# One Trainium2 core, a hybrid decoder layer: identity products in waits, upper expert weights loaded by halves, the output projection's second half in two passes, routing picks in pairs

## The chip, the cores and the metric

The kernel runs on one core of one Trainium2 chip. The metric is device time in microseconds (us) of one execution, the median of three. Lower is better. TensorE multiplies and transposes, VectorE (DVE) and ScalarE (ACT) work element by element, GpSimd (POOL) here adds and gathers rows by indirect transfers, and SyncE (SP) issues all other transfers in one queue.

## What is computed

One pre-norm decoder layer on 512 tokens of 1024 channels, in float32. Cut to what matters here:

```python
h = rmsnorm(x, g_mix); proj = h @ w_in            # attention, convolution, mLSTM and gates
merged = gate0*(y_att@w_br_att) + gate1*(y_conv@w_br_conv) + gate2*(y_m@w_br_mlstm)
x = x + merged @ w_out
h2 = rmsnorm(x, g_ffn)
lg = h2 @ w_router_g + b_router_g                 # top 1 of 4 groups
le = h2 @ w_router_e + b_router_e                 # top 2 of the 8 experts in it
x = x + moe(h2)                                   # 32 experts, 256 hidden, silu(x@gate)*(x@up) @ down
x = x + sigmoid(rmsnorm(x, g_ple) @ w_ple_gate) * (p @ w_ple_proj)
return rmsnorm(x, g_final)
```

## The kernel before, in words

Each engine has one hand-written program, and the engines meet at counting semaphores. Every engine runs strictly in its written order, so a wait holds all that stands behind it. Tokens are in T = 4 tiles of P = 128, channels in KD = 8 tiles. A float32 operand of a large product is split in a rounded high part and a remainder, and three products (high x high, low x high, high x low) replace one. ScalarE rounds, VectorE makes the remainder. A plain float32 product shows as two TensorE instructions in the profile.

**Start.** Token tiles are normed (`normed_tile`, VectorE L1679), transposed on TensorE (L1113) into eight PSUM banks, rounded by ScalarE (`h_rounding`, L713) and split by VectorE (`h_remainder`, L1687). `first_column_tile` then does its three groups of eight products, the last group on the remainders.

**Projection `merged @ w_out`.** `project(i)` makes tile `i % 4` of column half `i // 4` in 24 products: for each of three parts (merged high x weight high, merged high x weight remainder, merged remainder x weight high) eight channel tiles. VectorE adds the result to x (`add_x2`, L2012). `turn_half(i - 1)`, four transposes, and `router(i - 1)`, four products with the router's weights, stand inside the 24 products of tile i. Between them VectorE's `h2_half` (L2022) copies the transposed piece out of PSUM and multiplies it by `g_ffn`. ScalarE squares each half row and takes the root (L977, L982).

**Routing.** For each token tile VectorE forms the reciprocal root (`row_root`), then `pick(t)`: logits, best group, the two best experts, their one-hot rows `oh` and their sum `tmp`. `ranked` turns counts from TensorE (`RANKS`, `LAST_RANKS`) into places in the experts' blocks, and `hits` makes the table of token numbers. GpSimd gathers the rows by that table. `constant_products` are products of the identity with itself. Five 512-wide products stand before `HIT_WEIGHT`, the table of weights.

**Experts.** For n = 0 to 31: `up(n)` (16 products on 2 MB of weights), `turn_block(n + 1)` (four transposes of gathered rows, L1505), `expert_down(n - 1)` (1 MB of weights). Weights lie in a ring of RING = 7 slots for up and 9 for down. A slot is given back when its product is done (`up_done`, `down_done`), and SP then issues the next load into it:

```python
            for n in range(RING, NEXP):
                if DOWN_RING <= n < IN_ORDER:
                    sp.wait_ge(down_done, n + 1 - DOWN_RING)
                    down_weights(n)
                sp.wait_ge(up_done, n + 1 - RING)
                up_weights(n)
```

The slots lie over memory that earlier stages use. Slot 4 of up lies over `merged_low`, and slot 3 of down over channel tiles 4 to 7 of the second half's weight remainder, `wo_low[1]`. Before, both are loaded after the projection's last tile, from L569 and L572.

**Tail.** The per-layer embedding's products, the sum of the experts' rows read back, and two more norms.

Of the kernel before, what the change touches and what calls it, by code (L numbers as in the profile page):

```python
# [28 lines left out]
F32 = mybir.dt.float32  # L29
# [94 lines left out]
def build(nc, x, consts, chan, g_mix, r_bias, g_final, w_cm, w_tm, w_if, w_gate, w_branch, w_out,  # L124
# [5 lines left out]
    with ExitStack() as ctx:  # L130
# [115 lines left out]
        DOWN_RING, IN_ORDER = len(down_w), 20  # L246

# [61 lines left out]
        best_at = sb("best_at", [P, 8], mybir.dt.uint32)  # L309
        best_index = sb("best_index", [P, 8])  # L310
# [58 lines left out]
        w_if_split = sem("w_if_split")  # L369
        if_projected = sem("if_projected")  # L370
# [5 lines left out]
        columns_read = sem("columns_read")  # L376
# [14 lines left out]
        tm_done = sem("tm_done")  # L391
# [111 lines left out]
        def _(sp):  # L503
# [19 lines left out]
            def token_weights(r):  # L523

                sp.wait_ge(if_projected, 1)
                sp.dma_start(wtm, w_tm[r, :, :, :]).then_inc(tm_loaded, 16)
# [28 lines left out]
            sp.wait_ge(tm_done, ROUNDS * T)  # L555
# [39 lines left out]
            up_weights(3)  # L595

# [13 lines left out]
            down_weights(3)  # L610
            down_weights(4)
            up_weights_in_halves(4)
# [5 lines left out]
            for n in range(RING, NEXP):  # L618
# [3 lines left out]
                sp.wait_ge(up_done, n + 1 - RING)  # L622
                up_weights(n)
# [54 lines left out]
        def _(act):  # L678
# [48 lines left out]
            def forget_gate():  # L727

                act.wait_ge(if_projected, 1)
# [86 lines left out]
            def token_out(r, u):  # L816
                act.wait_ge(tm_done, r * T + u + 1)
# [154 lines left out]
            for i in range(2 * T):  # L972
                t, total = i % T, (square_halves, ss2)[i // T]
                act.wait_ge(x2_ready, i + 1 + (i == 2 * T - 1))
                if i:
                    act.wait_ge(x2_squared, i)
                act.activation(junk2, x_sb[:, t, i // T * 512:(i // T + 1) * 512], ACT.Square,  # L977
                               accum_out=total[:, t:t + 1]).then_inc(x2_squared, 1)
                if i >= T:
                    act.wait_ge(x2_squared, i + 1)  # L980
                    act.wait_ge(mean_ready, 1)
                    act.activation(rr2[:, t:t + 1], ss2[:, t:t + 1], ACT.Sqrt, scale=1.0 / D,  # L982
                                   bias=mean_halves[:, t:t + 1]).then_inc(rooted, 1)
            act.wait_ge(picked, T)
# [110 lines left out]
        def _(pe):  # L1095
# [13 lines left out]
            for t in range(T):  # L1109
                pe.wait_ge(x_normed, t + 1)  # L1110
# [21 lines left out]
            def gates():  # L1132

                pe.wait_ge(w_if_split, 1)
# [3 lines left out]
                last.then_inc(if_projected, 1)  # L1138
# [20 lines left out]
            def token_tile(r, u, first=0, end=KD):  # L1159
# [9 lines left out]
                if end == KD:  # L1169
                    last.then_inc(tm_done, 1)  # L1170
# [100 lines left out]
            def units(r):  # L1271

                if r == 0:
                    pe.wait_ge(columns_read, 1)
# [86 lines left out]

            def project(i, first=0, end=3 * KD):
# [5 lines left out]
                if i == T:  # L1368
                    pe.wait_ge(rounded, WO_REST_ROUNDED + KD)
                for n, (part, k) in list(enumerate(last_tile_last if i == 0 else by_part))[first:end]:  # L1370
# [6 lines left out]
                    if i == T and n == KD:  # L1377
# [3 lines left out]
                              n == 0, n == 3 * KD - 1)  # L1381
                if end == 3 * KD:
# [37 lines left out]
            pe.wait_ge(params_loaded, 32)  # L1420
            pe.wait_ge(gate_read, 3 * KD)
            project(0)
            for i in range(1, T + 1):
# [4 lines left out]
                project(i, 10)  # L1428
            for i in range(T + 1, 2 * T):
                project(i, 0, 4)  # L1430
                turn_half(i - 1)
                if i < 2 * T - 1:
                    project(i, 4, 10)
                else:
                    project(i, 4, 8)
                    pe.wait_ge(picked, 2)
                    mm(RANKS, const("upper"), tmp[:, 0:2, :], True, False)
                    mm(RANKS[:, NEXP:], ones, tmp[:, 0, :], False, True).then_inc(routing_mm, 1)
                    project(i, 8, 10)
                router(i - 1)  # L1440
                project(i, 10)
# [8 lines left out]
            constant_products(1)  # L1450
# [10 lines left out]
            pe.wait_ge(picked, 3)  # L1461
            mm(LAST_RANKS[:, NEXP:], ones, tmp[:, 2, :], False, False)
# [13 lines left out]
            pe.wait_ge(picked, T + 1)  # L1476
# [973 lines left out]
```

## Time and profile before

| | |
|---|---|
| median of 3 runs | 933.99 us (933.07 to 936.02) |
| the profiled execution's own time | 939.01 us |
| its span, first to last instruction | 937.1 us |
| TensorE busy | 896.6 us (96%) |
| VectorE busy | 503.9 us (54%) |
| ScalarE busy | 343.3 us (37%) |
| GpSimd busy | 195.6 us (21%) |
| mean granted TensorE clock | 0.988 |
| bytes moved | 180.35 MB, mean 192 GB/s |

The 1.9 us between the profiled time and its span lie outside the first and last instruction. TensorE's busy time is a modelled one: an engine shown busy can still run at the low clock or wait within a group. Rates of 410 to 430 GB/s are the highest that the core's transfers reach in the page's 40 slices.

### The profile page before, as it was taken

The numbers are of one execution on the slowest core, as the hardware profiler recorded it, in microseconds if no ns is written. First come the engines' busy times: TensorE is split into PE (matmuls) and PEld (weight loads), VectorE is DVE, ScalarE is ACT, GpSimd is POOL, SyncE is SP. The second block draws the span as 40 slices with busy tenths as digits, with TensorE's granted clock in tenths as the row PEclk, the third lists the DMA queues.
The fourth block names the chain that finished last, engine by engine and source line by source line (L and its number), as shares of the span: only waits on it lengthen the run. The fifth ranks groups of instructions, "written<-read, shape, count | busy, mean of one in ns | idle before, by whom it ended". The sixth has DMA issues, their size and how long they took to land. (4 is left out here: it accounts for less than half of the span.)

```text
span 937.1 us, 12264 instructions
## 1 busy us (share of the span) xinstructions
PE 896.6 (96%) x4816; PEld 658.4 (70%) x4816; DVE 503.9 (54%) x1043; ACT 343.3 (37%) x571; POOL 195.6 (21%) x169
## 2 busy tenths in 40 slices
PE   5999999999999999999999999998999999879896
PEld 4778778878877887888888888874555555434586
DVE  6368679759767999943333336474112112111766
ACT  5534453535355357622222243111122122112465
POOL 0052253327134433000000000001333332221000
PEclk9999999999999999999999999998999999999899
DMA  7430321121131111551222219969999999999701
GB/s 278 168 103 23 114 80 54 58 101 57 35 113 45 46 56 46 213 177 73 85 94 101 101 37 395 355 228 349 421 419 422 420 417 421 418 422 393 270 23 68
DMA packets 28801, 180.35 MB, mean 192 GB/s; under 512 B 5808, under 2 KB 6320, under 8 KB 17992
## 3 DMA queue, kind: packets, MB, share of 16 engines
q1 hardware_dynamic: 23624, 171.16, 46.3%
q0 software_dynamic: 5120, 8.41, 2.4%
q8 instruction: 39, 0.64, 0.3%
q14 instruction: 18, 0.15, 0.0%
HBM read 175.33 MB, written 12.59 MB: 201 GB/s over the span
## 5 line engine op out<-in xcount | busy, mean ns | idle before, releaser
L1097 PE MATMUL bank<-mT_parts,low_parts 128*128 128x512 f32 (+1 forms) x456 | 178.5, 394 | 0.0
L1097 PE MATMUL bank<-arena,cst 128*64 128x256 f32 (+2 forms) x918 | 135.9, 437 | 8.8 <-DMA arena<-in_w_expert 7.2
L1097 PE MATMUL bank<-mT_parts,x_parts 128*128 128x512 f32 (+1 forms) x328 | 132.7, 405 | 2.7 <-DVE arena L1766 2.3
L1097 PE MATMUL bank<-hT_parts,x_parts 128*128 128x512 f32 (+1 forms) x328 | 129.1, 394 | 0.0
L1701 DVE TENSOR_TENSOR low_parts<-arena,x_parts 128x1024 fp32r<-128x1024 f32 (+1 forms) x44 | 64.6, 1470 | 93.8 <-ACT x_parts L707 93.4
L2183 DVE TENSOR_TENSOR cst<-bank,chn 128x512 f32<-128x512 f32 x32 | 22.1, 692 | 168.1 <-PE bank L1505 168.1
L1097 PEld LDWEIGHTS bank<-arena,cst 128*64 128x64 f32 (+1 forms) x918 | 64.4, 141 | 64.6 <-issue 31.6
L1097 PEld LDWEIGHTS bank<-mT_parts,low_parts 128*128 128x128 f32 (+1 forms) x456 | 85.0, 186 | 21.2
L1753 DVE SCALAR_TENSOR_TENSOR arena<-arena,chn 128x512 f32<-128x512 f32 x116 | 99.1, 912 | 0.0
L2334 POOL DMA_INDIRECT mT<-x_rows,table x32 | 33.0, 1031 | 270.5 <-DVE table L2113 257.6
L1097 PE MATMUL bank<-arena 128*128 128x64 f32 (+9 forms) x400 | 79.8, 332 | 0.0
L1097 PEld LDWEIGHTS bank<-mT_parts,x_parts 128*128 128x128 f32 (+1 forms) x328 | 61.0, 186 | 19.6 <-DVE low_parts L1701 3.5
L2319 POOL TENSOR_TENSOR arena<-arena 128x128 f32<-128x128 f32 (+3 forms) x32 | 38.6, 1207 | 172.8 <-ACT arena L803 172.8
L1097 PEld LDWEIGHTS bank<-hT_parts,x_parts 128*128 128x128 f32 (+1 forms) x328 | 61.0, 186 | 15.3 <-issue 1.0
L1097 PEld LDWEIGHTS bank<-arena 128*128 128x128 f32 (+1 forms) x400 | 56.4, 189 | 19.6 <-issue 13.6
L2340 POOL DMA_INDIRECT expert_rows<-mT,table x32 | 32.4, 1013 | 152.0 <-ACT mT L1005 147.5
L803 ACT ACTIVATE arena<-arena,small 128x384 f32<-128x384 f32 (+3 forms) x32 | 32.6, 1020 | 56.9 <-DVE small L1853 56.9
L1097 PE MATMUL bank<-mT_parts,cm_high_b 128*128 128x512 f32 x128 | 52.4, 419 | 0.0
L948 ACT ACTIVATE arena<-bank 128x512 f32<-128x512 f32 x24 | 14.2, 595 | 101.6 <-PE bank L1097 94.6
L1097 PE MATMUL bank<-hT_parts,cm_high_b 128*128 128x512 f32 x128 | 49.2, 393 | 0.0
L1005 ACT ACTIVATE mT<-bank,table_weight 128x512 f32<-128x512 f32 x32 | 22.0, 687 | 67.0 <-PE bank L1097 67.0
L1097 PE MATMUL bank<-x_parts,mT_parts 128*128 128x384 f32 x128 | 44.8, 350 | 0.0
(303 smaller groups left out, 1582.0 us busy)
## 6 DMA issues: line engine op xcount, KB each, us to landing
arena<-in_w_expert SPq DMA_DIRECT2D x21, 2048.0 KB, 26.8
arena<-in_w_expert SPq DMA_DIRECT2D x26, 1024.0 KB, 23.9
arena<-in_w_cm SPq DMA_DIRECT2D x32, 512.0 KB, 3.5
arena<-in_w_gate SPq DMA_DIRECT2D x7, 1536.0 KB, 6.5
yT<-in_w_expert SPq DMA_DIRECT2D x5, 2048.0 KB, 23.2
hT<-in_w_expert SPq DMA_DIRECT2D x4, 2048.0 KB, 25.1
arena<-in_w_tm SPq DMA_DIRECT2D x4, 1536.0 KB, 6.9
arena<-in_w_branch SPq DMA_DIRECT2D x8, 768.0 KB, 7.8
```

Source lines behind the costliest of these rows:

```text
L803: act.activation(sc[:, u % 2, 0:n], sc[:, u % 2, 0:n], ACT.Exp, bias=nmx[:, u % 2:u % 2 + 1], accum_out=den[:, u:u + 1]).then_inc(exps_don ...
L948: act.activation(sgm[:, br], (PA, PB, S_16)[br][:, :], ACT.Sigmoid).then_inc(gate_read, 1)
L1005: act.activation(yr[slot], Y[b2][:, :], ACT.Copy, scale=table_w(0, n)).then_inc(y_scaled, 1)
L1097: return pe.matmul(out, lhsT, rhs, start=start, stop=stop)
L1701: dve.tensor_tensor(low, weights, high.bitcast(F32), ALU.subtract).then_inc(done, 1)
L1753: dve.scalar_tensor_tensor(cacc[:, j % 2], ypad[:, j:j + SEQ], weight, cacc[:, j % 2], ALU.mult, ALU.add).then_inc(conv_step, 1)
L2183: dve.tensor_tensor(xT[b2], TR[:, :].rearrange("p (k h s) -> p k h s", k=KD // 2, h=2), chn[:, G_FFN:G_FFN + KD].rearrange("p (h k) -> p k ...
L2319: pool.tensor_tensor(dst[:, 0:n], sc[:, u % 2, 0:n], sc[:, u % 2, n:2 * n], ALU.add).then_inc(pool_step, 1)
L2334: pool.indirect_dma_start(out=xr[slot], out_offset=None, in_=x2_halves, in_offset=bass.IndirectOffsetOnAxis(ap=token_halves, axis=0), boun ...
L2340: pool.indirect_dma_start(out=expert_halves, out_offset=bass.IndirectOffsetOnAxis(ap=row_halves, axis=0), in_=yr[slot], in_offset=None, bo ...
```

## The change

Six edits. (1) Before the transposes of token tiles 0 to 2, TensorE does 7, 6 and 3 identity products; 8 stand before the first `turn_block`, 4 behind it, and `constant_products(1)` before the last router becomes 2. (2) The second column half of the projection runs in two passes over its four tiles: first the 12 products that read `merged_low` and `wo_low[1]`'s upper half, then the other 12. `up_weights(4)` and `down_weights(3)` are issued behind the first pass. (3) Loads 7, 8 and 9 of the up ring are issued by halves, the first half when the first half of `up(0)`, `up(1)`, `up(2)` is done. (4) The transposed pieces are copied by ScalarE without a factor; `g_ffn` is multiplied once into the router's weights by VectorE, in the merge stage. (5) `pick` and `row_roots` handle two token tiles at a time: 0 and 1, then 2 and 3, the latter behind the last router. (6) The `RANKS` products move from the middle of the last projection tile to behind it, ahead of the last `turn_half`, and one product of `LAST_RANKS` moves behind `picked`.

```diff
             pe.wait_ge(ident_loaded, 16)
             for t in range(T):
+                for q in range((7, 6, 3, 0)[t]):
+                    mm(MM[:, 0:P], ident, ident)
                 pe.wait_ge(x_normed, t + 1)
...
+            low_first = [(2, k) for k in range(KD)] + [(1, k) for k in range(KD // 2, KD)]
+            second_half = low_first + [(1, k) for k in range(KD // 2)] + [(0, k) for k in range(KD)]
+            LOW = len(low_first)
...
-                project(i, 10)
+                project(i, 10, LOW if i == T else 3 * KD)
             for i in range(T + 1, 2 * T):
-                project(i, 0, 4)
-                turn_half(i - 1)
-                if i < 2 * T - 1:
-                    project(i, 4, 10)
-                else:
-                    project(i, 4, 8)
-                    pe.wait_ge(picked, 2)
-                    mm(RANKS, const("upper"), tmp[:, 0:2, :], True, False)
-                    mm(RANKS[:, NEXP:], ones, tmp[:, 0, :], False, True).then_inc(routing_mm, 1)
-                    project(i, 8, 10)
-                router(i - 1)
-                project(i, 10)
+                project(i, 0, LOW)
+            project(T, LOW)
+            project(T + 1, LOW, LOW + 5)
+            turn_half(T)
+            project(T + 1, LOW + 5)
+            project(T + 2, LOW, LOW + 1)
+            router(T)
...
+            project(T + 3, LOW + 5, LOW + 10)
+            pe.wait_ge(columns_then_logits_read, 2)
+            router(T + 2)
+            project(T + 3, LOW + 10)
+            pe.wait_ge(picked, 2)
+            mm(RANKS, const("upper"), tmp[:, 0:2, :], True, False)
+            mm(RANKS[:, NEXP:], ones, tmp[:, 0, :], False, True).then_inc(routing_mm, 1)
             constant_products(2)
             turn_half(2 * T - 1)
-            constant_products(1)
+            constant_products(2)
             router(2 * T - 1)
...
+            constant_products(8)
             turn_block(0, 0, rows_gathered[0], 16, first=True)
+            constant_products(4)
```

SyncE's part and the marks on TensorE:

```diff
+        IN_HALVES_FROM = (0, 1, 2)
+        IN_HALVES = (5,) + tuple(n + RING for n in IN_HALVES_FROM)
...
             def up_weights_in_halves(n):
                 for half in range(2):
+                    if n >= RING:
+                        sp.wait_ge(*((tm_then_up_half_done, ROUNDS * T + n + 1 - RING), (up_done, n + 1 - RING))[half])
...
             up_weights(2)
             up_weights(3)
+            sp.wait_ge(if_then_low_projected, 2)
+            up_weights(4)
+            down_weights(3)
...
-                sp.wait_ge(up_done, n + 1 - RING)
-                up_weights(n)
+                if n in IN_HALVES:
+                    up_weights_in_halves(n)
+                else:
+                    sp.wait_ge(up_done, n + 1 - RING)
+                    up_weights(n)
```

ScalarE's order for the last piece, and VectorE's for the pairs:

```diff
+            x2_square(2 * T - 1)
+            turned_copy(2 * T - 1, 0, 2, OUT, 2 * T)
+            x2_root(2 * T - 1)
+            turned_copy(2 * T - 1, 2, 4, S_16, 2 * T + 1)
...
-            for t in range(T - 1):
-                h2_half(T + t)
-                row_root(t)
-                if t == T - 2:
-                    ranked(0, RANKS, 1)
-                pick(t, lambda: add_x2(T + t + 1))
+            add_x2(T + 1)
+            row_roots(0)
+            add_x2(T + 2)
+            pick(0, lambda: add_x2(T + 3))
...
-            h2_half(2 * T - 1)
-            row_root(T - 1)
-            pick(T - 1, lambda: None)
+            ranked(0, RANKS, 1)
+            row_roots(T - 2)
+            pick(T - 2, lambda: None)
```

In the paired `pick` the reductions, the copy of the indices, the one-hot rows and `tmp` take both tiles in one instruction. The logits, the comparison with the best group, its one-hot row, the masked logits, the best eight and their indices stay one instruction for each tile.

## Rows read from the trace of the kernel before

**Rows 1.** The trace by windows: busy time of each engine, clock, transfers.

```profile
618.00:620.00 2.00, 2.00 (x14) 1.78 (x14) 1.80 (x7) 0.00 (x0) 0.00 (x0) 1.00 0.00 0
638.00:640.00 2.00, 1.00 (x4) 0.60 (x4) 0.11 (x1) 0.00 (x0) 0.00 (x0) 0.76 1.04 412
...
646.00:648.00 2.00, 1.50 (x14) 0.75 (x10) 0.47 (x1) 1.01 (x1) 0.00 (x0) 1.00 0.28 68
700.00:800.00 100.00, 100.00 (x718) 51.66 (x716) 18.36 (x47) 21.30 (x48) 32.69 (x32) 1.00 1.01 420
```

**Rows 2.** Timeline of the experts in mid-stage: start, duration, instruction.

```profile
691.23 0.66 PE L1505 MATMUL bank<-cst,mT 128*128 128x128 f32 x4
697.55 0.66 PE L1505 MATMUL bank<-cst,mT 128*128 128x128 f32 x4
```

**Rows 3.** Timeline of SP, its load issues around the experts' start.

```profile
593.89 0.80 SPq L564 DMA_DIRECT2D arena<-in_w_expert  x2
...
624.97 3.33 SPq L569 DMA_DIRECT2D arena<-in_w_expert  x4
...
646.94 0.33 SPq L564 DMA_DIRECT2D arena<-in_w_expert  x1
```

**Rows 4.** Timeline of the start, transposes and first column tile.

```profile
2.09 0.43 SPq L509 DMA_DIRECT2D cst<-in_consts  x1
...
9.09 1.94 PE L1113 MATMUL bank<-cst,arena 128*128 128x128 f32 x8 [9.09 <-DVE arena L1679]
...
15.11 3.67 PE L1113 MATMUL bank<-cst,arena 128*128 128x128 f32 x16 [0.81 <-DVE arena L1679]
...
18.70 3.24 PE L1097 MATMUL bank<-mT_parts,cm_high_b 128*128 128x512 f32 x8
...
19.69 2.47 DVE L1687 TENSOR_TENSOR hT_parts<-bank,mT_parts 128x512 fp32r<-128x512 f32 x4
...
23.65 2.03 PE L1097 MATMUL bank<-hT_parts,cm_high_b 128*128 128x512 f32 x8
```

**Rows 5.** Timeline of the last projection tile and last pick.

```profile
617.14 0.53 PE L1097 MATMUL bank<-tmp,cst 128*128 128x64 f32 x4
...
622.47 0.75 DVE L2012 TENSOR_TENSOR x_sb<-x_sb,bank 128x256 f32<-128x256 f32 x2 [0.59 <-PE bank L1097]
622.95 0.77 PE L1405 MATMUL bank<-cst,x_sb 128*128 128x128 f32 x4
...
624.01 0.29 ACT L982 ACTIVATE small<-small 128x1 f32<-128x1 f32 x1
...
625.44 0.25 DVE L2059 SCALAR_TENSOR_TENSOR rl<-bank,small,r_b 128x36 f32<-128x36 f32 x1
...
626.38 0.23 DVE L2063 TENSOR_SCALAR t<-rl,per 128x4 f32<-128x4 f32 x1
626.51 0.22 DVE L2066 TENSOR_SCALAR oh<-oh,per 128x4 f32<-128x4 f32 x1
...
628.00 0.25 DVE L2075 SCALAR_TENSOR_TENSOR tmp<-cst,best_index,oh 128x32 f32<-128x32 f32 x1
...
628.31 0.43 PE L1097 MATMUL bank<-tmp,cst 128*128 128x64 f32 x2 [0.82 <-DVE tmp L2075]
```

**Rows 6.** The page's groups, ScalarE's copy of a bank.

```profile
L948 ACT ACTIVATE arena<-bank 128x512 f32<-128x512 f32 x24 | 14.2, 595 | 101.6 <-PE bank L1097 94.6
```

**Rows 7.** Timeline from the routing's fillers to expert 1.

```profile
631.44 4.54 PE L1097 MATMUL bank<-cst 128*128 128x512 f32 x10
...
635.91 1.15 PE L1097 MATMUL bank<-mT,cst 128*64 128x64 f32 x32
...
638.85 1.00 PE L1505 MATMUL bank<-cst,mT 128*128 128x128 f32 x4 [1.79 <-DMA mT<-x_rows,table]
...
640.73 6.18 PE L1097 MATMUL bank<-arena,cst 128*64 128x256 f32 x32 [0.88 <-DVE cst L2183]
...
648.37 1.95 PE L1097 MATMUL bank<-yT,cst 128*64 128x256 f32 x16 [0.88 <-DVE cst L2183]
```

More of the change, by code:

```diff
@@ L246, in build, with up_count @@
         DOWN_RING, IN_ORDER = len(down_w), 20
+        IN_HALVES_FROM = (0, 1, 2)
+        IN_HALVES = (5,) + tuple(n + RING for n in IN_HALVES_FROM)
+        def up_count(n):
+            return sum(16 * (1 + (m in IN_HALVES)) for m in range(n % RING, n + 1, RING))
         CM_LOADS = 2 * ROUNDS * 16
@@ L971, in _, with x2_square @@
             wo_rounding(1, 0, KD)
-            for i in range(2 * T):
+            def x2_square(i):
                 t, total = i % T, (square_halves, ss2)[i // T]
@@ L978, in _, with x2_root, turned_copy @@
                                accum_out=total[:, t:t + 1]).then_inc(x2_squared, 1)
-                if i >= T:
[L980 to L984, printed above, removed]
+            def x2_root(i):
+                t = i - T
+                act.wait_ge(x2_squared, i + 1)
+                act.wait_ge(mean_ready, 1)
+                act.activation(rr2[:, t:t + 1], ss2[:, t:t + 1], ACT.Sqrt, scale=1.0 / D,
+                               bias=mean_halves[:, t:t + 1]).then_inc(rooted, 1)
+            def turned_copy(i, first, end, bank, count):
+                act.wait_ge(x2_turned, count)
+                if i and first == 0:
+                    act.wait_ge(logits_done, i)
+                act.activation(h2_piece[:, first:end, :], bank[:, 0:(end - first) * P].rearrange("p (k s) -> p k s", k=end - first),
+                               ACT.Copy).then_inc(h2_ready, 1)
+            for i in range(2 * T - 1):
+                x2_square(i)
+                turned_copy(i, 0, 4, (S_16, OUT)[i % 2], i + 1)
+                if i >= T:
+                    x2_root(i)
+            x2_square(2 * T - 1)
+            turned_copy(2 * T - 1, 0, 2, OUT, 2 * T)
+            x2_root(2 * T - 1)
+            turned_copy(2 * T - 1, 2, 4, S_16, 2 * T + 1)
+            act.wait_ge(picked, 3)
             act.activation(t4[:, :, :], t4[:, :, :], ACT.Exp).then_inc(act_step, 1)
@@ L1367, in project @@
                     pe.wait_ge(x2_ready, i - 3)
-                if i == T:
+                if i == T and first == 0:
                     pe.wait_ge(rounded, WO_REST_ROUNDED + KD)
-                for n, (part, k) in list(enumerate(last_tile_last if i == 0 else by_part))[first:end]:
+                order = second_half if i >= T else last_tile_last if i == 0 else by_part
+                for n, (part, k) in list(enumerate(order))[first:end]:
                     if i == 0 and part == 0:
@@ L1381, in project @@
                               n == 0, n == 3 * KD - 1)
+                if i == 2 * T - 1 and end == LOW:
+                    last.then_inc(if_then_low_projected, 1)
                 if end == 3 * KD:
@@ L1476, in _ @@
             pe.wait_ge(picked, T + 1)
+            mm(LAST_RANKS[:, NEXP:], ones, tmp[:, 2, :], False, False)
             mm(LAST_RANKS, const("upper"), tmp[:, 2:T, :], False, True).then_inc(routing_mm, 1)
@@ L1512, in up @@
                 for k in range(KD):
+                    if k == KD // 2 and in_halves:
+                        last.then_inc(tm_then_up_half_done, 1)
                     if k == KD // 2 and between:
```

164 lines of the change are left out of this document (97 added, 67 removed).

## The prediction

> **What bounds the kernel now.** I read three views in turn: the busy shares, the trace by windows, and the timelines of the three places that the change touches. TensorE is busy for 96% of the span, so up to the experts whatever shortens TensorE's line shortens the kernel. In the experts' stage it is the loads: over 700 to 800 us transfers run at 420 GB/s with nothing to spare [rows 1]. An expert needs 3 MB (2 for up, 1 for down), some 7.5 us at that rate, while TensorE takes one expert every 6.32 us [rows 2]. TensorE lives on the slots filled in advance and must run out of them. So the end of that stage is fixed by when the stream of loads starts to run without a break, and not by when TensorE starts. The reader should see in [rows 1] two holes in the stream: none moved at 618 to 620, and 68 GB/s at 646 to 648. In the second, all slots were full and SP could issue nothing before up(0) had ended; the next load goes out at 646.94 [rows 3]. That instant is the one to follow. All loads before it are worth nothing, as long as they have landed by then.
>
> **The start.** Sixteen transposes take 3.67 us in the start [rows 4], 0.23 each, where four take 0.66 with their tail in mid-stage [rows 2], and the first eight products of the first column tile take 3.24 against 2.03 for the last eight [rows 4]. TensorE is at the low of its two clocks, 1.2 GHz, until some 21 us; the window rows do not say so there, the durations do. Ten fillers of 512 columns take 4.54 us [rows 7], so an instruction of 128 columns costs some 0.11 and an identity product, two such, 0.21 at the high clock and 0.43 at the low one. Seven products can begin once the identity is there (issued at 2.09), in front of the transposes of 9.09. If they bring the high clock, VectorE's last remainder, which ends at 19.69 + 2.47 = 22.16 [rows 4], becomes what the third group waits for: its last four products take 1.0, and with the second group in front the tile ends near 23.6 instead of 23.65 + 2.03 = 25.7, less a tail of 0.2. **Gain 1.9.** Lower bound none, if the clock rises no earlier.
>
> **First column half.** ScalarE copies the transposed pieces in place of VectorE. A copy of 512 columns takes 0.60 [rows 6]. ScalarE must square the half row first, and for tile 0 it is still rounding weights, so the first router waits some 0.25; the later ones have room. VectorE's new product on the router's weights lies in the merge stage, under TensorE's work: nothing; without that cover it would be some 0.4. **Cost 0.25.**
>
> **Second half and the pair.** The same number of products runs. Moving RANKS out of the last tile takes some 0.4 out ahead of the last add (four instructions, 0.53 with tail [rows 5]), which then ends at 622.47 + 0.75 - 0.4 = 622.8. But TensorE now waits for pick(0)'s tmp before the last transposes, and pick(0) puts that add in its middle: behind it come two one-hot operations and tmp, three steps of some 0.2, so 623.45. Then RANKS 0.4 and two identity products 0.4: the last transposes start at 624.25 instead of 622.95 [rows 5]. What is late next is ScalarE. It copies half a piece (between half and all of 0.60 [rows 6]; I take 0.4) and only then takes the root: at 625.15 instead of 624.01 [rows 5]. The reciprocal root has one operation more, 0.2, so the last pick starts 1.3 late, at 626.75 instead of 625.44.
>
> In the pick, an operation that waits for none follows in 0.13 (626.38 to 626.51 [rows 5]); a chained one costs 0.2 to 0.3. Added are five unchained seconds (0.65), two instructions for the second index search (0.25), one chained step for the first half's logits (0.3), and the second one-hot operation in front of tmp (0.2): 1.4. tmp starts at 628.00 + 2.7, and a product of 0.1 stands behind it ahead of the ranks. The table of tokens, the gathers and HIT_WEIGHT are all 2.85 late. **Cost 2.85**, bounds 2.0 (the pairs overlap more) and 3.6 (every added operation at 0.25).
>
> The Trainium skill (ScalarE: Activation LUTs, What ACT_TABLE_LOAD costs) gives a copy with immediate scale 186 ns plus 0.833 ns a column. For 512 columns that is 0.61 and [rows 6] agree; for 256 it is 0.40, the value taken between the bounds above. At the bound of 0.60 the cost would be 3.05.
>
> **Start of the experts.** HIT_WEIGHT ended at 637.06 [rows 7], now at 639.9. Eight products take 1.7, to 641.6, just the time at which the gathered rows would come if they need as long as before (638.85 + 2.85). So the eight products hide in that wait. If the rows come earlier, because the stream is empty then, the products cost what they overhang, at most 1.7, but nothing is gained either, since they stand in line in front. The transposes fell into a low clock: 0.76 over 638 to 640 [rows 1], 1.00 for four against 0.66, and up(0) took 6.18 against twice 1.95 [rows 7]. With the waits filled, up(0) starts at 641.7 + 1.88 - 0.34 = 643.25 and its first half ends at 645.2. In the start's time, 645.2 - 1.9 + 0.25 = 643.55. SP issues half of load 7 then: 3.4 before 646.94.
>
> **The loads put forward.** up 4 and down 3 go out behind the first pass, near 606.5 (593.89 plus the last turn and router of the first half and 48 products of 0.23), not at 624.97 and after [rows 3]. Without that, some 7.5 MB issued from 623.7 on would end at 643 or later and hold the stream; with it, 4.5 MB are left and end near 635. It gains nothing by itself; it lets the earlier release count. On SP's queue the two stand ahead of the stores of x2, which wait for VectorE anyhow until 610. On the freed stream half a slot of 1 MB lasts 2.5 us, and the next halves come a little late once: **cost 0.35.** Later releases follow TensorE, itself 1.5 earlier. **Gain of the release 3.05 in all**, start, first half and routing included.
>
> **The term that I cannot read off.** While VectorE does the longer pick, TensorE has only the ranks of two tiles, hits(0, 2) and three products. Before, it idled 0.82 there [rows 5]; now 0.82 + 1.4 for the pair and some 0.3 for ScalarE's root coming behind the copy: 2.5 us. In the trace an idle stretch of 1.79 was followed by the low clock [rows 7], and the next was 4 us of work at low clock, which cost up(0) 2.3 us. Behind the new gap stand hits, totals and five long fillers that end exactly when HIT_WEIGHT may start, so the low clock delays HIT_WEIGHT, the eight products and up(0). Bounds: 0, if the clock holds, and 3.4, half of the some 6.8 us that it was low around up(0). Nearest is the 2.3; part of the low time falls into waits this time, so I take 1.7. **Cost 1.7.**
>
> The Trainium skill (TensorE: Matmul & The Clock Gate, Part 1) says that the low clock is the default and sustained activity releases it, and that a wait can bring it back. Both stretches above agree with it, 638.85 with a granted 0.76. It speaks for the products in the start and against the longer gap at the pick; without the fall the sum would be 930.9, with it 932.6.
>
> **Sum.** -3.05 + 1.7 = -1.35. Of the profiled execution's 939.01 that leaves 937.7. The median of the runs shown is 5.0 lower, 933.99; nothing in the sum depends on what the profiler adds, so 932.6.
>
> **Rivals.** *The clock holds in the gap.* For it: three products stand at the gap's edge and the work before it is dense. Against it: the 1.79 us gap. -3.05: 930.9. *More than that*, if the pair costs only 2.0 as well: 929.5 to 930.
>
> *The start goes the other way.* At the low clock seven products take 3.0, six 2.6, three 1.3, and end behind the normed tiles they should fill in for (9.09; then 0.81 of idle before 15.11 [rows 4]). If the clock stays low all the same, the transposes of tiles 2 and 3 end 2.4 later and the first column tile some 1.3 later. It decides once the high clock comes later than 15 us. In place of -1.9 stands +1.3: +1.85, 935.8, or 937.5 with the full 3.4 for the gap. Against it: products fill the waits without a break from 7 us on, in the before they had three idle stretches.
>
> *The stream's end is not moved*, because something behind it (the scatter of the last expert, the rows read back) has its own clock: 934.0. Against it: all of it follows the last down.
>
> *Split loads cost.* Three loads more are in the queue. The trace shows 420 GB/s over a hundred us of back-to-back loads [rows 1], so no price while others are queued. The Trainium skill (DMA: Bandwidth & Descriptors, Anatomy of one DMA) puts a fixed cost of about 2 us on each transfer. By that figure, shown three times over, the time would be 938.6, an estimate from the page. From rows: each first half meets an empty stream and its start-up shows. Load 7, issued at 646.94, had moved 0.3 us' worth (68 of 420 GB/s over 2 us [rows 1]) by 648, so it starts some 0.8 us after its issue; three times that is +2.4: 935.0.
>
> **How the numbers follow.** Forecast 0.42 (its own range 930.7 to 934.3), clock holds 0.24, more than that 0.10, start reversed 0.12, end not moved 0.08, split loads 0.04. No change is told from 933.99 within 0.3%, 2.8 us: faster is below 931.2, slower above 936.8. Faster: 0.17 of the second, all of the third and 0.08 of the first, 0.35. Slower: 0.05 of the fourth, 0.02 of the last and 0.07 of the others' far ends, 0.14. The rest is 0.51. The range from 929.2 to 936.5 leaves out the far end on either side, some 0.1 each.
>
> **What would show each step.** Start: the group on the remainders ends near 23.6, and eight transposes take 1 us. Pick: the last tmp 2.7 after its old place, counted from the last add. Gap: windows of 2 us between 628 and 640 with a clock below 1.00, and five fillers that take more than 4.54. Release: the first half-load issued 1.5 to 3.5 before 646.94, with TensorE at high clock in up(0), and no hole between. Experts: TensorE waits for weights from some 800 us on as before. I am wrong if the transposes at the start end later than 18.8, if TensorE starts the experts later than 641 in its own time, or if the gathered rows come late for another reason.

## The result, and the profile after

The changed kernel takes 938.77 us (median of 13 executions, 936.28 to 942.6). The kernel before, timed beside it on the same chip, takes 934.16 (13 executions, 932.24 to 936.73). The ratio is 1.0051, with a 95% interval of 1.0039 to 1.0063: **slower by 0.5%**, and outside the range of 929.2 to 936.5 that was forecast. The profiled execution of the changed kernel took 938.91 us. That is hardly less than the 939.01 of the one profiled before, so the two traces side by side hide the loss. Why they do is the second thing that the runs showed. One execution of the run `edges_only` below took 1786.45 us: its median includes it, its ratio does not.

The page of the changed kernel, its line of engines:

```profile
PE 901.3 (96%) x4874; PEld 664.5 (71%) x4874; DVE 493.7 (53%) x1013; ACT 347.4 (37%) x580; POOL 195.5 (21%) x169
```

TensorE is busy 4.7 us longer than before (896.6). The line numbers have moved: the products are L1131 (L1097 before), `turn_half` L1448, `turn_block` L1556, `tmp` L2162, the loads by halves L577. Its timeline in the start, to be held against [rows 4]:

```profile
10.41 1.38 PE L1149 MATMUL bank<-cst,arena 128*128 128x128 f32 x8
...
15.02 2.29 PE L1149 MATMUL bank<-cst,arena 128*128 128x128 f32 x16 [0.35 <-DVE arena L1734]
...
17.66 2.11 PE L1131 MATMUL bank<-mT_parts,cm_high_b 128*128 128x512 f32 x8 [0.34 <-ACT mT_parts L725]
...
21.71 2.03 PE L1131 MATMUL bank<-hT_parts,cm_high_b 128*128 128x512 f32 x8
```

The sixteen transposes take 2.29 us instead of 3.67, the first group 2.11 instead of 3.24, and the last group starts at 21.71 instead of 23.65: 1.94 earlier. This part did what it was meant to do.

The timeline around the routing, to be held against [rows 5] and [rows 7]:

```profile
619.98 0.75 DVE L2072 TENSOR_TENSOR x_sb<-x_sb,bank 128x256 f32<-128x256 f32 x2 [0.60 <-PE bank L1131]
...
621.39 0.63 PE L1131 MATMUL bank<-tmp,cst 128*128 128x64 f32 x4 [1.52 <-DVE tmp L2162]
...
622.66 1.06 PE L1448 MATMUL bank<-cst,x_sb 128*128 128x128 f32 x4
...
624.37 1.52 PE L1131 MATMUL bank<-wr_sb,cst 128*128 128x36 f32 x8
...
626.01 0.42 DVE L2131 SCALAR_TENSOR_TENSOR rl<-bank,small,r_b 128x36 f32<-128x36 f32 x2 [1.05 <-PE bank L1131]
...
630.06 0.66 PE L1131 MATMUL bank<-tmp,cst 128*128 128x32 f32 x4 [2.22 <-DVE tmp L2162]
...
632.60 1.92 PE L1131 MATMUL bank<-tmp,cst 128*128 128x32 f32 x8
634.33 6.92 PE L1131 MATMUL bank<-cst 128*128 128x512 f32 x10
641.19 1.15 PE L1131 MATMUL bank<-mT,cst 128*64 128x64 f32 x32
...
644.16 0.60 PE L1556 MATMUL bank<-cst,mT 128*128 128x128 f32 x4
...
645.63 3.67 PE L1131 MATMUL bank<-arena,cst 128*64 128x256 f32 x32
647.61 0.33 SPq L577 DMA_DIRECT2D arena<-in_w_expert  x1
```

Each pair's pick now holds TensorE once: 1.52 us for tiles 0 and 1, 2.22 for tiles 2 and 3, where the one wait before was 0.82 [rows 5]. Behind each, the same work takes longer than at the high clock: `turn_half` 1.06, the router 1.52 and `totals` (the eight products of 632.60) 1.92, against 0.60, 1.06 and 1.08 in the run with both waits filled below, and the five long fillers 6.92 against 4.54 [rows 7]. The last add is 2.49 earlier than before (619.98 against 622.47), the start of `up(0)` is 4.90 later (645.63 against 640.73). The waits of TensorE for the two picks stand in one row (sum, number, longest):

```profile
PE bank L1131 <- DVE tmp L2162: 3.7, 2, 2.2
```

The windows give the granted clock (the third figure from the end) and what the transfers move (the last, in GB/s):

```profile
622.00:624.00 2.00, 2.00 (x12) 2.00 (x12) 1.08 (x4) 0.67 (x3) 0.00 (x0) 0.52 0.86 281
624.00:626.00 2.00, 2.00 (x14) 2.00 (x13) 0.82 (x6) 1.45 (x2) 0.00 (x0) 0.63 1.03 422
...
632.00:634.00 2.00, 2.00 (x23) 1.88 (x23) 0.28 (x1) 0.00 (x0) 0.09 (x1) 0.58 1.00 422
634.00:636.00 2.00, 2.00 (x5) 1.15 (x5) 1.30 (x5) 0.00 (x0) 1.69 (x2) 0.50 0.95 391
636.00:638.00 2.00, 2.00 (x4) 0.79 (x3) 1.69 (x10) 0.00 (x0) 1.47 (x2) 0.50 0.50 152
638.00:640.00 2.00, 2.00 (x5) 0.94 (x4) 1.72 (x6) 0.00 (x0) 0.99 (x1) 0.71 0.35 82
640.00:642.00 2.00, 2.00 (x30) 1.00 (x30) 0.00 (x0) 0.00 (x0) 0.00 (x0) 1.00 0.07 23
```

There are two falls to 1.2 GHz, one behind each wait. In all these windows TensorE is busy throughout: a reader who goes by the busy share alone sees nothing. The stream of loads thins from 636 on and stands still by 644, ahead of the first half-load of 647.61. The Trainium skill (TensorE: Matmul & The Clock Gate, Part 1) has the low clock as the state to which the engine falls back when it idles. The level agrees (0.52 and 0.50). What the Trainium skill warns of there are longer waits than these two; here the runs decide.

### The profile page after: what moved, and what is told of

Its sections match the earlier page's. It is cut to its first block and busy times, and to the rows that moved or that the text cites. A ratio compares the mean times of both kernels' runs of the same rounds, so it can differ in the third digit from the quotient of the medians.

```text
span 936.9 us, 12359 instructions
## 1 busy us (share of the span) xinstructions
PE 901.3 (96%) x4874; PEld 664.5 (71%) x4874; DVE 493.7 (53%) x1013; ACT 347.4 (37%) x580; POOL 195.5 (21%) x169
## 5 line engine op out<-in xcount | busy, mean ns | idle before, releaser
L1131 PE MATMUL bank<-mT_parts,low_parts 128*128 128x512 f32 (+1 forms) x456 | 178.6, 394 | 0.0
L1131 PE MATMUL bank<-arena,cst 128*64 128x256 f32 (+2 forms) x918 | 131.8, 426 | 5.2 <-DMA arena<-in_w_expert 4.5
L1131 PE MATMUL bank<-mT_parts,x_parts 128*128 128x512 f32 (+1 forms) x328 | 132.7, 405 | 2.8 <-DVE arena L1821 2.3
L1131 PE MATMUL bank<-hT_parts,x_parts 128*128 128x512 f32 (+1 forms) x328 | 129.1, 394 | 0.0
L1131 PEld LDWEIGHTS bank<-arena,cst 128*64 128x64 f32 (+1 forms) x918 | 62.9, 137 | 58.5 <-issue 27.8
L1131 PEld LDWEIGHTS bank<-mT_parts,low_parts 128*128 128x128 f32 (+1 forms) x456 | 84.9, 186 | 21.5 <-DVE low_parts L1756 0.4
L1131 PE MATMUL bank<-arena 128*128 128x64 f32 (+9 forms) x400 | 79.8, 332 | 0.0
L1131 PEld LDWEIGHTS bank<-mT_parts,x_parts 128*128 128x128 f32 (+1 forms) x328 | 61.0, 186 | 19.6 <-DVE low_parts L1756 3.5
L1131 PEld LDWEIGHTS bank<-hT_parts,x_parts 128*128 128x128 f32 (+1 forms) x328 | 61.0, 186 | 15.3 <-issue 1.0
L1131 PEld LDWEIGHTS bank<-arena 128*128 128x128 f32 (+1 forms) x400 | 56.4, 189 | 19.6 <-issue 13.6
L1131 PE MATMUL bank<-mT_parts,cm_high_b 128*128 128x512 f32 x128 | 51.2, 409 | 0.3 <-ACT mT_parts L725 0.3
L1131 PE MATMUL bank<-hT_parts,cm_high_b 128*128 128x512 f32 x128 | 49.2, 393 | 0.0
L1131 PE MATMUL bank<-x_parts,mT_parts 128*128 128x384 f32 x128 | 44.8, 350 | 0.0
```

Of the source, the lines that this page charges most:

```text
L1131: return pe.matmul(out, lhsT, rhs, start=start, stop=stop)
```

## The experiments

All ratios are to the kernel before, run beside each kernel on the same chip, with a 95% interval in brackets. A ratio is not the quotient of two medians: the two differ by up to 0.2%. So medians of different sets are compared with care, since the kernel before itself has medians of 933.8, 933.9, 935.7 and 934.5 in the four sets.

**The kernel before once more.**

> The kernel before, unchanged, to get a profile nearer its median (the first profile took 939.0 us, its runs 934.2). Both theories: ratio 1.000 within 0.2%. If the profile shows about 934 us, the missing 5 us must lie in one stage: theory A (low clock around the experts' start) expects up(0) faster than 6.2 us and the next load issued 1 to 2 us before 646.9; theory B (the stream of loads) expects the same start and the experts' end earlier than 859.7.

Median 934.15, ratio 0.9999 (0.9984 to 1.0014). Its profiled execution took 935.0 us, 4.0 less than the one of the page before. Its timeline around the experts' start, to be held against [rows 7]:

```profile
635.79 1.15 PE L1097 MATMUL bank<-mT,cst 128*64 128x64 f32 x32
...
638.76 0.66 PE L1505 MATMUL bank<-cst,mT 128*128 128x128 f32 x4 [1.82 <-DMA mT<-x_rows,table]
...
640.30 3.67 PE L1097 MATMUL bank<-arena,cst 128*64 128x256 f32 x32 [0.87 <-DVE cst L2183]
...
644.00 0.33 SPq L564 DMA_DIRECT2D arena<-in_w_expert  x1
...
857.10 7.13 PE L1097 MATMUL bank<-hT 128*128 128x512 f32 x16 [0.38 <-DMA hT<-in_pT]
```

After the same wait for the gathered rows (1.82 against 1.79) `up(0)` takes 3.67 here and 6.18 in the execution of [rows 7]. The low clock that the prediction set out to remove is there in one of the two executions whose trace is kept. The times of the others say that the kernel before has short and long executions: of the 140 in these sets, 46 have a mean granted clock of 0.992 or less and take 936.8 us on average (935.93 to 939.05), and the 62 at 0.997 or more take 933.1. Whether the low clock of the 46 lies at `up(0)` too is not shown. The median is that of an execution outside this third. The last row is the first product of the layer embedding, which marks the experts' end.

**The start alone.**

```diff
             for t in range(T):
+                for q in range((7, 6, 3, 0)[t]):
+                    mm(MM[:, 0:P], ident, ident)
                 pe.wait_ge(x_normed, t + 1)
```

> The kernel before with the 7, 6 and 3 identity products in the start alone. The changed kernel's trace has the last group of the first column tile 1.9 us earlier. Theory A: that gain reaches the end, -1.3 to -1.9 us (ratio 0.998). Theory B: it is lost again by the experts' stage, within 0.5 us of none.

Median 933.59, ratio 0.9994 (0.9979 to 1.0008). The last group of the first column tile starts at 21.70, `up(0)` at 638.71, 1.6 before that of the unchanged kernel, and the load at 642.42, likewise. The experts' end is at 856.40, 0.7 earlier, and the ratio does not tell that from nothing.

**The start and the experts' edge:** the start's products, those around the first `turn_block`, and loads 7, 8 and 9 by halves. Pairs, passes, early loads and ScalarE's copies are left out.

```diff
+            constant_products(8)
             turn_block(0, 0, rows_gathered[0], 16, first=True)
+            constant_products(4)
...
-                sp.wait_ge(up_done, n + 1 - RING)
-                up_weights(n)
+                if n in IN_HALVES:
+                    up_weights_in_halves(n)
+                else:
+                    sp.wait_ge(up_done, n + 1 - RING)
+                    up_weights(n)
```

> The kernel before with the start's products, the 8 and 4 products around the first turn_block, and loads 7, 8, 9 by halves; without the two passes, the early loads, ScalarE's copies and the pairs. Theory A (the pairs and their clock falls cost, the rest gains): -2 to -4 us, the release held by the loads issued late, near 645. Theory B (halves or the products before turn_block cost): no gain or a loss of 1 to 3 us.

Median 933.92, ratio 0.9984 (0.9968 to 1.0001); a repeat in another set gave 933.94, 0.9993 (0.9980 to 1.0006). Released at 640.42, the experts end at 855.03 in a trace taken of one of its shortest executions (930.98). Together the two say that these parts are harmless and may gain some 0.1%, which is not shown: both intervals reach 1. What does stand out is the long third of the kernel before: none of the other 23 executions of this kernel takes more than 935.50.

> edges_only once more, beside the other two, since its interval touched 1. Theory A: ratio 0.997 to 0.999, under 1 with its interval. Theory B: 1.000.

**The changed kernel with both waits filled.** It has fifteen identity products more than the changed kernel, and nothing else differs:

```diff
+            for q in range(5):
+                mm(S_1[:, 0:P], ident, ident)
             pe.wait_ge(picked, 2)
...
             hits(0, 2, True, False)
-            constant_products(3)
+            constant_products(13)
```

> The changed kernel with 5 identity products ahead of the wait in front of RANKS and 10 more behind hits(0, 2). Theory A (the clock falls in those two waits and costs the time): granted clock 1.00 from 600 to 650, fillers 4.5 us again, up(0) starts near 643.3, and 2 to 3 us less than the changed kernel, near 936. Theory B (the clock is not what costs): within 1 us of the changed kernel.

Median 934.13, ratio 0.9999 (0.9986 to 1.0012). More work for TensorE makes the kernel 4.6 us faster by the medians, which are of two sets, and 0.5% by the ratios (0.4% against the repeat of the changed kernel below). Its timeline:

```profile
631.65 4.54 PE L1131 MATMUL bank<-cst 128*128 128x512 f32 x10
636.12 1.15 PE L1131 MATMUL bank<-mT,cst 128*64 128x64 f32 x32
...
639.09 0.60 PE L1558 MATMUL bank<-cst,mT 128*128 128x128 f32 x4
...
640.57 3.67 PE L1131 MATMUL bank<-arena,cst 128*64 128x256 f32 x32
...
642.54 2.05 SPq L577 DMA_DIRECT2D arena<-in_w_expert  x2
...
856.81 7.13 PE L1131 MATMUL bank<-hT 128*128 128x512 f32 x16 [0.41 <-DMA hT<-in_pT]
```

Its windows hold 1.00 where the changed kernel had 0.58 and 0.71:

```profile
632.00:634.00 2.00, 2.00 (x6) 0.88 (x5) 1.76 (x8) 0.00 (x0) 1.64 (x2) 1.00 1.03 434
...
638.00:640.00 2.00, 2.00 (x21) 2.00 (x20) 0.27 (x1) 0.00 (x0) 0.00 (x0) 1.00 0.16 47
```

`up(0)` starts 5.06 earlier than in the changed kernel and the experts end 4.31 earlier (856.81 against 861.12). The two falls of the clock are the whole loss, as far as the interval tells.

**One wait filled at a time.** First only the five products ahead of `pe.wait_ge(picked, 2)`, then only the ten more behind `hits(0, 2)`.

> The changed kernel with only the first of the two waits filled: 5 products ahead of the wait in front of RANKS. Theory A (either wait brings the clock down, and the later fall meets the long fillers): the fall near 622 is gone, the one near 632 stays, fillers still over 4.5 us; 1 us less than the changed kernel, near 937.8. Theory B (the first fall is what costs): near 934.5.

Median 937.09, ratio 1.0030 (1.0013 to 1.0047), for the first wait filled.

> The changed kernel with only the second wait filled: 10 more products behind hits(0, 2). Theory A: fillers 4.54 us again, up(0) near 641.5, and 3 us less than the changed kernel, near 935.5; the low clock near 622 to 626 costs 1 us in the last transposes and router. Theory B (the first fall costs most): near 938.

Median 936.41, ratio 1.0018 (1.0001 to 1.0035), for the second. The long fillers and `up(0)`, of the first and then of the second:

```profile
633.75 7.14 PE L1131 MATMUL bank<-cst 128*128 128x512 f32 x10
...
645.27 3.67 PE L1131 MATMUL bank<-arena,cst 128*64 128x256 f32 x32
```

```profile
622.85 1.06 PE L1448 MATMUL bank<-cst,x_sb 128*128 128x128 f32 x4
...
633.64 4.54 PE L1131 MATMUL bank<-cst 128*128 128x512 f32 x10
...
642.56 3.67 PE L1131 MATMUL bank<-arena,cst 128*64 128x256 f32 x32
```

With the second wait left open the first fall is gone and the second is there (7.14), and the other way round (`turn_half` 1.06, fillers 4.54). From the first pair's `RANKS` to `up(0)` it takes 19.40 us with both filled (621.17 to 640.57), 20.93 with the first open, 23.76 with the second open and 24.24 with both. So the traces, one of each kernel, give the second wait 4.4 alone and the first 1.5. The ratios give them 0.3% and 0.2%, which add up to the 0.5%. How it is shared is less certain than that: the interval of the first kernel overlaps that of the changed one (1.0039 to 1.0063), and both overlap that of its repeat.

**The first wait taken away by order.** The ten products stay, and the `RANKS` of the first pair move behind the last `turn_half`:

```diff
             project(T + 3, LOW + 10)
-            pe.wait_ge(picked, 2)
-            mm(RANKS, const("upper"), tmp[:, 0:2, :], True, False)
-            mm(RANKS[:, NEXP:], ones, tmp[:, 0, :], False, True).then_inc(routing_mm, 1)
             constant_products(2)
             turn_half(2 * T - 1)
+            pe.wait_ge(picked, 2)
+            mm(RANKS, const("upper"), tmp[:, 0:2, :], True, False)
+            mm(RANKS[:, NEXP:], ones, tmp[:, 0, :], False, True).then_inc(routing_mm, 1)
-            constant_products(2)
+            constant_products(1)
```

> The changed kernel with the second wait filled, and with the wait for the first pair and the RANKS products behind the last turn_half instead of ahead of it. Theory A (that wait holds up the last transposes, and everything behind them): last transposes 1.2 to 1.7 us after the end of the projection earlier, first half-load issued near 641.3, the median 0.5 to 1.5 below gaps_filled (ratio 0.998 to 0.999). Theory B (the stream is full to 637 and the gather sets the start): the same as gaps_filled.

Median 933.98, ratio 0.9998 (0.9982 to 1.0013). The last transposes come 1.2 earlier than with the filled waits (620.91 against 622.16), but the load goes out at 642.85 against 642.54: nothing is won. VectorE's timeline says why:

```profile
623.15 0.42 DVE L2108 TENSOR_TENSOR cst<-per,cst 128x256 f32<-128x256 f32 x1
623.50 0.15 DVE L2081 SCALAR_TENSOR_TENSOR small<-small 128x2 f32<-128x2 f32 x1
...
624.55 0.42 DVE L2131 SCALAR_TENSOR_TENSOR rl<-bank,small,r_b 128x36 f32<-128x36 f32 x2
```

VectorE ends `ranked(0)` only at 623.57, since it needs the `RANKS` that now come later, and `row_roots` and the last pick stand behind it in written order. So earlier transposes alone do not bring the last pick forward: another wait took the place of the first.

**Filled waits, without the eight products ahead of the first `turn_block`.**

```diff
-            constant_products(8)
             turn_block(0, 0, rows_gathered[0], 16, first=True)
```

> gaps_filled without the 8 products in front of the first turn_block. Theory A (the gathered rows come as late as before, the products only fill): no difference in the start of turn_block, 639.0, and the clock may fall in up(0), +0 to +2 us. Theory B (the stream is empty there, the rows come early, and the products overhang): turn_block 0.5 to 1.7 us earlier.

Median 932.94, ratio 0.9984 (0.9967 to 1.0001). The first `turn_block` waits for the rows again:

```profile
636.53 1.15 PE L1131 MATMUL bank<-mT,cst 128*64 128x64 f32 x32
...
640.23 0.66 PE L1558 MATMUL bank<-cst,mT 128*128 128x128 f32 x4 [2.55 <-DMA mT<-x_rows,table]
640.73 1.88 PE L1131 MATMUL bank<-cst 128*128 128x128 f32 x8
642.53 4.46 PE L1131 MATMUL bank<-arena,cst 128*64 128x256 f32 x32
```

The eight products thus lie in that wait, as forecast, and no cost of theirs shows. In this execution the clock fell behind the wait (1.88 against 1.06, 4.46 against 3.67) and the experts end at 860.86. It is also the longest of the ten (938.39), and seven of the others take 933.83 or less: behind this wait too the fall is not there every time. That the products gain something is not shown: the two medians differ by 1.2 us, of different sets, and the intervals of the ratios overlap.

**Filled waits, loads at their old place.** `up_weights(4)` and `down_weights(3)` are issued behind the last tile, as before, but for `up_weights(4)` being one load and not two halves.

```diff
-            sp.wait_ge(if_then_low_projected, 2)
-            up_weights(4)
-            down_weights(3)
...
             store_x2(T - 1)
+            down_weights(3)
             down_weights(4)
+            up_weights(4)
```

> gaps_filled with up 4 and down 3 issued behind the last tile, as before the change. Theory A (the early loads only move the hole in the stream): the hole of 637 to 643 is gone, the stream is full from 624 on, and the time is within 1 us of gaps_filled. Theory B (the early loads are what lets the early release count): 1 to 3 us more than gaps_filled.

Median 936.22, ratio 1.0004 (0.9988 to 1.0020). The stream is full to 642 (408 GB/s over 640 to 642) and the load goes out at 643.81, 1.3 later than with the early loads. The ratios do not tell the two apart.

**Filled waits, loads 7, 8 and 9 whole.**

```diff
-        IN_HALVES_FROM = (0, 1, 2)
+        IN_HALVES_FROM = ()
```

> gaps_filled with loads 7, 8 and 9 whole, each when its up is done. Theory A (the release sets the experts' end when the stream is empty): the first load goes out 1.95 us later, near 644.5, and the time is 1.5 to 2 us more than gaps_filled, near 936. Theory B (split loads cost their start-up): the same or less.

Median 935.19, ratio 0.9992 (0.9978 to 1.0006). The release and the experts' end:

```profile
644.94 0.33 SPq L570 DMA_DIRECT2D arena<-in_w_expert  x1
...
857.79 7.13 PE L1131 MATMUL bank<-hT 128*128 128x512 f32 x16 [0.38 <-DMA hT<-in_pT]
```

With halves the first load goes out 2.40 earlier (642.54). Of this 0.66 is a later start of `up(0)` in this execution (641.23 against 640.57), and 1.74 is the halves. The experts' end is 0.98 earlier only, and the ratios (0.9992 and 0.9999) show neither a gain nor a cost of the halves.

**A version without pairs and passes, loads put forward in another way.** On top of the start and the experts' edge, the last projection tile alone does its reads of `merged_low` first, and the two loads go out within it:

```diff
+            sp.wait_ge(if_projected, 2)
+            up_weights(4)
+            down_weights(3)
             sp.wait_ge(x2_mm, 2 * T)
             store_x2(T - 1)
-            down_weights(3)
             down_weights(4)
-            up_weights_in_halves(4)
```

> edges_only, and the last projection tile alone in the order of the first pass, so that up 4 and down 3 are issued some 4 us before its end; picks still one tile at a time. Theory A (edges_only was held by the loads issued late): loads done near 639, the half-load at 640.4 finds an empty stream, 1 to 2 us less than edges_only, ratio 0.995 to 0.998. Theory B (the experts' end follows something else): the same as edges_only, 0.998.

Median 935.54, ratio 0.9998 (0.9980 to 1.0017). `hits` with the three identity products behind it, and GpSimd's first gather in this kernel:

```profile
624.42 2.64 PE L1110 MATMUL bank<-cst 128*64 128x64 f32 x22
...
632.04 1.25 POOL L2359 DMA_INDIRECT mT<-x_rows,table  x1 [259.36 <-DMA x_rows<-x_sb]
```

What releases the gathers is no longer the table but the store of x2, issued at 621.79 behind 3 MB of weights on the same queue. A second thing shows in this trace: over 624 to 628 the clock is low (0.63 and 0.51), though TensorE has not waited longer than 0.31 since the last projection tile. So a fall can come without a wait like those above. For the next kernel only `up_weights(4)` was left ahead of that store, with `down_weights(3)` behind it.

> last_tile with down 3 issued behind the store of the last x2 tile, so that only 2 MB lie ahead of the store. Theory A (in last_tile the store landed behind 3 MB of weights and the gathers waited for it): the gathers wait for the table again, the transposes of the first block start near 637, 3 us earlier than in last_tile, and the median is 1 to 3 us below the kernel before, ratio 0.997 to 0.999. Theory B (the experts' end does not follow its start): ratio 1.000 as last_tile.

Median 932.73, ratio 0.9980 (0.9963 to 0.9997). `hits`, the gather and the experts' end:

```profile
624.08 1.55 PE L1110 MATMUL bank<-cst 128*64 128x64 f32 x22
...
629.98 1.25 POOL L2359 DMA_INDIRECT mT<-x_rows,table  x1 [257.65 <-DVE table L2138]
...
855.01 7.13 PE L1110 MATMUL bank<-hT 128*128 128x512 f32 x16 [0.38 <-DMA hT<-in_pT]
```

The table releases the gather again. It comes 2.06 earlier than in the kernel above: the table is written 0.60 earlier (628.79 against 629.39, `hits` being at the high clock here), and the other 1.46 is the store. The ratio is 0.2% below 1, and this is the one version whose interval lies below 1. Its upper end is 0.9997, and among fifteen ratios one such interval can come by chance.

**The changed kernel once more.**

> The changed kernel once more on this chip: ratio 1.004 to 1.006, with a clock below 1.00 in the stretch 620 to 640 in its profile; if it comes out within 0.2% of the kernel before, the loss belongs to the chip and not to the kernel.

Median 937.99, ratio 1.0037 (1.0020 to 1.0055): the loss repeats in another set, a little smaller than expected. In its profiled execution the clock held over 622 to 624 (1.00) in spite of a first wait of 1.51, and fell behind the second:

```profile
633.25 6.28 PE L1131 MATMUL bank<-cst 128*128 128x512 f32 x10
...
643.90 3.67 PE L1131 MATMUL bank<-arena,cst 128*64 128x256 f32 x32
```

## Why the prediction failed

**The start: right.** Forecast 1.9, measured 1.94 (1.6 against the second execution of before).

**Second half and last pick: right up to the router.** The last add starts 2.49 earlier (forecast 1.9 - 0.25 + 0.4 = 2.05), the last transposes at 622.66 (622.6 after the same shift of 1.65), the root at 623.61 (623.5). ScalarE's half copy, taken as 0.4, took 0.38. The last pick starts at 626.01 against 625.1, and there VectorE has waited 1.05 for a router that ran at the low clock.

**The pair: right in kind, too dear.** With the clock held, `up(0)` starts at 640.57, and with only the start changed at 638.71. All of pairs, passes, copies and `RANKS` together cost 1.9 there, against 2.85 + 0.25 = 3.1 (the 0.4 for `RANKS` is within the 2.85), so they were put 1.2 too high, and below their lower bound of 2.0 + 0.25.

**The release:** half of the load goes out 1.98 after the start of `up(0)`, as forecast (1.95), with `up(0)` at 3.67.

**The step that failed first is the term "that I cannot read off".** The mechanism was right: a longer wait in the pick brings the low clock, which delays `HIT_WEIGHT`, the eight products and `up(0)`. The size was wrong: 1.7 was taken, with 3.4 as the upper bound, and it measured 5.06 at the start of `up(0)` and 4.31 at the experts' end. One of the prediction's own signs of being wrong came: the experts start at 645.63, later than 641. Two things made it small. The prediction looked at one wait and one fall. But TensorE also waits for the first pair's `tmp`, which the working had, and this wait (1.52) was long enough for a fall of its own. And it let part of the low time fall into waits. There was hardly any: against the filled waits the last `tmp` comes 1.76 later (630.06 against 628.30, behind the slow router), `totals` take 0.84 more and the five fillers 2.38 more, 4.98 together.

**The second failing step is "nothing in the sum depends on what the profiler adds".** The sum was made against the one execution profiled before, in which `up(0)` itself ran at the low clock (6.18) and the release came at 646.94. The second execution had 3.67 and 644.00. So 2.94 of the gain of 3.05 was the removal of something that the other kept execution, 0.9 us above its median, does not have. Made against the other execution, the sum would have been -0.11 + 1.7, some 935.6 us, and 938.9 with the 5.06. That this meets the measured 938.77 is in part luck, since two more errors nearly cancel: the pair put 1.2 too high, and 1.1 lost at the start and behind the release. The difference of 5.0 us between that execution and the median was the sign, and it was read as the profiler's.

**The third term is the release itself: an earlier one was counted in full,** less a hole of 0.35 for the halves. Counted from the release to the experts' end, the four traces with whole loads take 212.9 to 214.0 (860.10 - 646.94 = 213.2 in the first), the twelve with halves 213.5 to 215.6, on average 0.9 more. So of the 1.7 by which a half goes out earlier about half reaches the end. But whole loads lose too: with the start alone the release is 1.58 earlier and the end 0.70. With the waits filled the release is 1.46 earlier than in the second execution of before, and the end 0.29, so 1.2 is lost where 0.35 was charged. What takes the difference was not found, and it is not the halves alone.

**The rivals.** "The clock holds" is what the filled waits make true, and it gave 934.1 and not 930.9: 2.94 for the execution that was taken as the base, 0.3 for the start (1.6 against 1.9) and 0.8 for what is lost behind the release beyond the 0.35, less the 1.2 by which the pair was put too high, make 2.8 of the 3.2. "Split loads cost" has no support as written: whole loads and halves have ratios of 0.9992 and 0.9999, with overlapping intervals. The estimate of 938.6 in that rival lies near the measured 938.77 by chance, since the filled waits keep all three halves and take 934.13; the section that it names for its 2 us (the Trainium skill, DMA: Bandwidth & Descriptors, Anatomy of one DMA) is on GpSimd's path, and these loads are SyncE's. "Start reversed" did not come. "The stream's end is not moved" is wrong for a late release, which the end follows (644.00 to 857.10, 647.61 to 861.12), and half right for an early one (1.58 gives 0.70).

**The account.** Against the second execution of before, the experts end 4.02 later: 4.31 from the clock, and -0.29 from all the rest. The medians say 4.6 in all.

**What stays open.** The start's 1.6 us reach the release in full, but the end by 0.7 and the ratio by 0.06% (-0.21 to 0.08). What takes the rest was not found. How often each of the two falls comes is open too: in one execution of two the first did not, and with `last_tile` one came without a long wait. The clock also falls behind the experts, in most of the sixteen kept traces: over 870 to 885 its mean is 1.00 in four, 0.89 in eight and 0.77 in four, and from the experts' end to the last instruction these take 73.8 to 74.2, 75.3 to 75.9 and 76.5 to 77.0 us. So one execution differs from the next by up to 3 us there (the two of the kernel before by 1.1), and the long third of the kernel before may come from it as well as from `up(0)`.

## What to carry to other kernels

Before a sum is made against a profiled execution, hold its time against the median; if it is several us above, look for a low clock that only some executions have, and count its removal as a gain by their share only. When an edit makes the wait of an otherwise dense TensorE longer, even by one or two us, count everything behind it at the low clock to the next slack, or put identity products in front of the wait: here fifteen of them were worth 0.4 to 0.5%. A load put forward past a small store on the same queue can hold whoever needs that store: 3 MB did here, 2 MB did not.

## What was not expected of the hardware

Waits of 1.52 and 2.22 us in a dense stretch brought TensorE to 1.2 GHz, for some 3 and 7 us of work behind them (clock 0.52 and 0.63; 0.58, 0.50, 0.50, 0.71). In the kernel before a wait of 1.8 did so in one execution (`up(0)` 6.18) and not in another (3.67), and in the changed kernel the first wait did so in one execution and not in its repeat. In `last_tile` it fell with no wait above 0.31 since the last projection tile, and in `one_load_early`, whose TensorE has the same work there, it did not (the products of `hits` take 2.64 and 1.55). So the clock behind a short wait is not a property of the kernel alone, and the wait is not all that decides. The 2 MB and 1 MB of weights ahead of a small store on SP's queue held back what waits for that store until 632.04, some 10 us after its issue at 621.79 and 2.65 after the table was written; with 1 MB of it moved behind the store, the gather followed the table by 1.19.
